# Order of work at the two seams between a LayerNorm stage and the feed-forward network of a hybrid decoder step

## What is computed

```python
def _swiglu(x, w_gate, w_up, w_down):
    return (jax.nn.silu(x @ w_gate) * (x @ w_up)) @ w_down

# layer 0: h = pooling mixer(x);  layer 1: h = latent attention(x) @ wo
x = _layer_norm(ALPHA * x + h, ln_g[l, 0], ln_b[l, 0])
x = _layer_norm(ALPHA * x + _swiglu(x, w_gate[l], w_up[l], w_down[l]), ln_g[l, 1], ln_b[l, 1])
```

## Time and profile before

| | |
|---|---|
| median of three runs | 2610.28 us |
| the profiled execution | 2611.03 us |
| its span, first to last instruction | 2609.2 us |
| mean granted TensorE clock | 0.969 |
| TensorE busy | 2415.3 us (93%) |
| VectorE busy | 1294.6 us (50%) |
| ScalarE busy | 769.7 us (30%) |
| GpSimd busy | 347.1 us (13%) |
| share of the chain that ended last, TensorE | 80% |

### The profile page before, as it was taken

How to read it: one execution, slowest core, us unless ns; L and a number is a source line. 1 busy time by engine, 2 the same in 40 slices (tenths; PEclk the granted TensorE clock), 3 DMA queues, 4 the chain that set the end, 5 groups by cost and what they waited for, 6 DMA issues and landing times.

```text
span 2609.2 us, 35320 instructions
## 1 busy us (share of the span) xinstructions
PE 2415.3 (93%) x14022; PEld 2198.0 (84%) x14022; DVE 1294.6 (50%) x2467; ACT 769.7 (30%) x1469; POOL 347.1 (13%) x308
## 2 busy tenths in 40 slices
PE   7899999999999768999998888898999999999994
PEld 7799999999999667898987667687999989999993
DVE  4623433333333765677767778643234434433336
ACT  2331111111111233555546556412311111111112
POOL 2400000000000330000006545032000000000006
PEclk9899999999999888999999999899999999999997
DMA  4021111111111031000004444500211111101111
GB/s 158 26 65 49 49 48 35 29 48 48 48 49 41 20 121 44 18 14 5 11 21 158 155 152 152 179 25 25 65 49 49 34 49 49 50 30 36 49 41 65
DMA packets 137082, 153.99 MB, mean 59 GB/s; under 512 B 10256, under 2 KB 114224, under 8 KB 136808
## 3 DMA queue, kind: packets, MB, share of 16 engines
q1 hardware_dynamic: 124656, 110.07, 13.4%
q0 software_dynamic: 12288, 41.95, 5.1%
HBM read 142.24 MB, written 10.32 MB: 58 GB/s over the span
## 4 chain that ended last, share of the span: by engine, by line
PE 80%; DVE 9%; ACT 4%; issue 3%; POOL 2%; DMA 2%; SPq 0%; POOLq 0%; ACTq 0%; DVEq 0%
PE ps L214 23%; PE ps L216 22%; PE ps L215 22%; DVE split L207 4%; ACT split L202 2%; PE ps L2010 2%; PE ps L2045 2%; POOL plain L338 1%; POOL plain L340 1%; PE ps L2025 1%; PE ps L222 1%; PE ps L221 1%; PE ps L2026 1%; PE ps L2032 1%; PE ps L1555 1%
## 5 line engine op out<-in xcount | busy, mean ns | idle before, releaser
L214 PE MATMUL ps<-split 128*128 128x512 f32 (+6 forms) x3632 | 1244.5, 343 | 69.9 <-DVE split L207 23.6
L215 PE MATMUL ps<-split 128*128 128x512 f32 (+6 forms) x3632 | 1229.2, 338 | 0.0
L216 PE MATMUL ps<-split 128*128 128x512 f32 (+6 forms) x3632 | 1228.1, 338 | 0.0
L214 PEld LDWEIGHTS ps<-split 128*128 128x128 f32 x3632 | 694.5, 191 | 120.1 <-DVE split L207 28.9
L216 PEld LDWEIGHTS ps<-split 128*128 128x128 f32 x3632 | 694.8, 191 | 38.0
L215 PEld LDWEIGHTS ps<-split 128*128 128x128 f32 x3632 | 694.8, 191 | 37.1
L202 ACT ACTIVATE split<-plain 128x1024 fp32r<-128x1024 f32 (+8 forms) x446 | 313.3, 738 | 628.7 <-PE ps L222 406.1
L207 DVE TENSOR_TENSOR split<-plain,split 128x1024 fp32r<-128x1024 f32 (+7 forms) x422 | 355.7, 867 | 193.1 <-ACT split L202 190.2
L274 DVE TENSOR_TENSOR plain<-plain,ps 128x512 f32<-128x512 f32 (+2 forms) x396 | 268.6, 685 | 201.9 <-PE ps L216 196.6
L910 DVE TENSOR_TENSOR plain<-plain,ps 128x350 f32<-128x350 f32 (+1 forms) x132 | 68.1, 516 | 574.6 <-ACT plain L866 574.0
L207 DVE TENSOR_TENSOR split<-ps,split 128x512 fp32r<-128x512 f32 (+5 forms) x480 | 247.6, 555 | 153.9 <-ACT split L202 146.4
(11 more groups left out here) (145 smaller groups left out, 1427.1 us busy)
## 6 DMA issues: line engine op xcount, KB each, us to landing
plain<-w_gate SPq DMA_DIRECT2D x44, 512.0 KB, 4.7
plain<-w_up SPq DMA_DIRECT2D x44, 512.0 KB, 4.0
plain<-w_down SPq DMA_DIRECT2D x44, 512.0 KB, 4.4
plain<-x_prompt SPq DMA_DIRECT2D x8, 512.0 KB, 11.2
x_spill<-plain SPq DMA_DIRECT2D x1, 4096.0 KB, 18.6
plain<-wo SPq DMA_DIRECT2D x8, 512.0 KB, 4.9
plain<-x_spill SPq DMA_DIRECT2D x8, 512.0 KB, 7.7
y_prompt<-plain SPq DMA_DIRECT2D x8, 512.0 KB
```

What stands on the lines that cost most here:

```text
L214: pe.matmul(out, still[0], moving[0], start=start, stop=False)
L215: pe.matmul(out, still[0], moving[1], start=False, stop=False)
L216: return pe.matmul(out, still[1], moving[0], start=False, stop=stop)
```

## The change

- The first three gate-and-up products are placed in steps 8, 9 and 11 of the normalising stage, ahead of the transposes of those steps, and the order of the six products of step 0 is part by part: (slot 0, part 0), (slot 1, part 0), (slot 0, part 1), (slot 1, part 1), and so on. The first waits for the transposed tiles 0 to 2, the second for those to 5, the fifth for all.
- Products with even numbers take banks 2 and 3, those with odd numbers 0 and 1. In mix and att the ring of the transposes shrinks to banks 0 and 1; tiles 6 and 7 use 7 and 4, the tail 5, with waits for their earlier users.
- Tiles 2 and 3 of the weights are split in step 8 of the normalising stage. The Silu, multiplication and splits of the first two products are done in steps 10 and 11, ahead of the transposed tiles of those steps on ScalarE.
- Tiles 4 and 5 are split ahead of the sixth product's Silu, since slot 0 is now read until the fifth product.
- The nine residual scalings go in threes behind the fourth, fifth and sixth products' Silus.

```diff
-def turn_bank(k, t, b):
-    if t >= k.tiles - 1:
-        return 7 if t == k.tiles else 2 + b
-    return (2 * t + b) % TURN_BANKS
+def turn_bank(k, ph, t, b):
+    if ph == "ffn0":
+        if t >= k.tiles - 1:
+            return 7 if t == k.tiles else 2 + b
+        return (2 * t + b) % TURN_BANKS
+    if t >= k.tiles - 2:
+        return 5 if t == k.tiles else (7, 4)[b]
+    return b
+
+def pe_turn_free(pe, k, ph, t, b):
+    n = 2 * t + b
+    if ph == "ffn0":
+        if n >= TURN_BANKS:
+            pe.wait_ge(*k.s.at(ph + "_turned_lo", n + 1 - TURN_BANKS))
+        return
+    if t == k.tiles:
+        pe.wait_ge(*k.s.at(ph + "_unit_taken", 2 * k.tiles + 1))
+        return
+    if n == 2 * (k.tiles - 2) and ph == "mix":
+        pe.wait_ge(k.s["pooled_lo"], 2 * k.tiles + 1)
+    if n == 2 * (k.tiles - 2) + 1:
+        pe.wait_ge(*k.s.at(ph + "_unit_taken", 2 * k.tiles))
+    if n >= 2:
+        pe.wait_ge(*k.s.at(ph + "_turned_lo", n - 1))
...
     def between(step):
-        if step >= k.tiles + 2:
-            k.ffn[layer].first_product(pe, step - k.tiles - 2)
+        if step in FIRST_PRODUCTS:
+            k.ffn[layer].gate_up(pe, 0, FIRST_PRODUCTS.index(step))
     return between
+
+FIRST_PRODUCTS = (8, 9, 11)
+
+def first_hidden(k, eng, layer, step, act):
+    if step in (10, 11):
+        (k.ffn[layer].act_hidden if act else k.ffn[layer].dve_hidden)(eng, 0, 0, step - 10)
...
         if step == k.tiles - 2:
             k.ffn[layer].split_first(eng, act)
+        if step == k.tiles:
+            if layer == 1 and act:
+                eng.wait_ge(*k.s.at("att_unit_done", 2 * (k.tiles + 1)))
+            k.ffn[layer].split_gate_up(eng, 0, 2, 1, 1, act)
+        first_hidden(k, eng, layer, step, act)
...
+def gu_bank(g, m):
+    return (2, 0)[g % 2] + m
...
+        if isinstance(st, int) and st == 0:
+            return [(0, 0), (1, 0), (0, 1), (1, 1), (0, 2), (1, 2)]
+        return [(slot, p) for slot in range(2) for p in range(PARTS)]
...
-            eng.wait_ge(*self.k.s.at(self.name("gu_done"), PARTS * c - PARTS))
+            eng.wait_ge(*self.k.s.at(self.name("gu_done"), 5 if isinstance(c, int) and c == 2 else PARTS * c - PARTS))
...
-        if isinstance(st, int) and st == 0 and slot == 0:
-
-            pe.wait_ge(*k.s.at(self.x_ph + "_turned_lo", (2 * k.tiles - 2, 2 * k.tiles, 2 * k.tiles + 1)[p]))
+        slot, p = self.order(st)[g]
+        if isinstance(st, int) and st == 0:
+
+            if g == 0 and self.layer == 0:
+                pe.wait_ge(k.s["pooled_lo"], 2 * k.tiles + 2)
+            if g in (0, 1, 4):
+                pe.wait_ge(*k.s.at(self.x_ph + "_turned_lo", {0: 6, 1: 12, 4: 17}[g]))
...
         def body(st, par):
+            first = isinstance(st, int) and st == 0
+            for g in range(2 if first else 0, 2 * PARTS):
+                if g == 0:
+                    self.weights(act, st, 0, True)
+                if g == (5 if first else PARTS):
+                    self.weights(act, st, 1, True)
+                self.act_hidden(act, st, par, g)
+                if first:
+                    for t in ((), (), (), (0, 1, 2), (3, 4, 5), (6, 7, 8))[g]:
+                        scale_row(t)
```

More of the change, by code:

```diff
@@ L676, in h_view, with order, h_count @@
         return self.k.h_tail[:, par, slot, part * LO:part * LO + b - a]
-    def h_count(self, q):
-        chunk, r = q // PARTS, q % PARTS
-        return (PARTS + 1) * chunk + r + 1 + (r == PARTS - 1)
+    def order(self, st):
+        if isinstance(st, int) and st == 0:
+            return [(0, 0), (1, 0), (0, 1), (1, 1), (0, 2), (1, 2)]
+        return [(slot, p) for slot in range(2) for p in range(PARTS)]
+    def h_count(self, st, q):
+        if q < 0:
+            return q
+        return sum(len(self.pieces(p)) for _, p in self.order(st)[:q + 1])
     def steps_of(self, eng, body, last):
@@ L809, in gate_up @@
             for kc in range(k.kc):
-                mm = product(pe, ps[:, 2 * (g % 2) + m, 0:b - a],
+                mm = product(pe, ps[:, gu_bank(g, m), 0:b - a],
                              (self.wgu(st, slot, m, 0)[:, kc, :], self.wgu(st, slot, m, 1)[:, kc, :]),
@@ L841, in body @@
         def body(st, par):
[L842 to L845, removed]
+            for g in range(len(FIRST_PRODUCTS) if isinstance(st, int) and st == 0 else 0, 2 * PARTS):
+                self.gate_up(pe, st, g)
             if isinstance(st, int) and st == 0:
@@ L853, in pe, with act_hidden @@
                                                       self.layer == 0, self.latent_products(pe)))
+    def act_hidden(self, act, st, par, g):
+        k = self.k
+        slot, p = self.order(st)[g]
+        n = 2 * PARTS * st + g
+        a, b = self.part(p)
+        act.wait_ge(*self.k.s.at(self.name("gu_done"), n + 1))
+        if not (isinstance(n, int) and n < 2):
+            act.wait_ge(*self.k.s.at(self.name("h_mul"), n - 1))
+        act.activation(k.silu[:, g % 2, 0:b - a], k.ps[:, gu_bank(g, 0), 0:b - a], ACT.Silu).then_inc(self.s("silu"), 1)
+        act.wait_ge(*self.k.s.at(self.name("h_mul"), n + 1))
+        if not (isinstance(st, int) and st < 2) and g == 0:
+            act.wait_ge(*self.k.s.at(self.name("unit_done"), 18 * (st - 1)))
+        for piece in self.pieces(p):
+            hi_part(act, self.h_view(par, 0, slot, piece), k.hidden[:, g % 2, piece[1]:piece[2]])\
+                .then_inc(self.s("h_hi"), 1)
@@ L856, in act @@
     def act(self, act):
         k, nt = self.k, self.nt
[L859 to L875, removed]
@@ L877, in body, with scale_row @@
-        def body(st, par):
[L878 to L890, removed]
+        def scale_row(t):
+            row = rows_of(k, t, nt)
+            if t == 0:
+                act.wait_ge(*k.s.at(self.x_ph + "_turned", 17))
+            act.activation(row, row, ACT.Copy, scale=ALPHA).then_inc(self.s("x_scaled"), 1)
@@ L897, in act, with dve_hidden @@
         self.steps_of(act, body, last)
+    def dve_hidden(self, dve, st, par, g):
+        k = self.k
+        slot, p = self.order(st)[g]
+        n = 2 * PARTS * st + g
+        a, b = self.part(p)
+        dve.wait_ge(*self.k.s.at(self.name("silu"), n + 1))
+        if not (isinstance(n, int) and n < 2):
+            dve.wait_ge(*self.k.s.at(self.name("h_lo"), 2 * (PARTS + 1) * st + self.h_count(st, g - 2)))
+        dve.tensor_tensor(k.hidden[:, g % 2, 0:b - a], k.silu[:, g % 2, 0:b - a], k.ps[:, gu_bank(g, 1), 0:b - a],
+                          ALU.mult).then_inc(self.s("h_mul"), 1)
+        dve.wait_ge(*self.k.s.at(self.name("h_hi"), 2 * (PARTS + 1) * st + self.h_count(st, g)))
+        for piece in self.pieces(p):
+            lo_part(dve, self.h_view(par, 1, slot, piece), k.hidden[:, g % 2, piece[1]:piece[2]],
+                    self.h_view(par, 0, slot, piece)).then_inc(self.s("h_lo"), 1)
@@ L900, in dve @@
     def dve(self, dve):
         k, nt = self.k, self.nt
[L903 to L918, removed]
-        def body(st, par):
[L921 to L925, removed]
+        def body(st, par):
+            first = isinstance(st, int) and st == 0
+            for g in range(2 if first else 0, 2 * PARTS):
+                if g == 0:
+                    self.weights(dve, st, 0, False)
+                if g == (5 if first else PARTS):
+                    self.weights(dve, st, 1, False)
+                self.dve_hidden(dve, st, par, g)
```

27 lines of the change are left out of this document (9 added, 18 removed).

## The result

The changed kernel takes 2588.33 us (median of 5 runs, 2584.85 to 2591.22), the kernel before beside it 2610.28 us. The ratio is 0.9922, 95% interval 0.9909 to 0.9935. The profiled execution took 2584.85 us with a span of 2583.0 us.

A forecast was written before the change was run, and what follows sets the result against it. TensorE bounds the kernel, busy at full clock in the steady feed-forward, with waits and half clock at the two seams. Gains 5.1 + 8.5 + 4.9 + 4.9 = 23.4 us give 2587 us, range 2576 to 2600.

The forecast's parts named there:

- The clock: Seams: half clock costs 2.7 us at layer 0's second product, 1.5 at each layer's third, none at layer 1's second.
- Start of the second product: Layer 0's seam: starts at 109.6 us after 6.1 us idle, split pair 5.9 us; layer 1: 2.3 us idle.
- Start of the third: Both seams: released by the first product's multiplication, 5.3 us after tile 6's transposes begin; 122.6 us in layer 0.
- Start of step 1: Waits of 3.7 and 3.8 us go, 0.3 and 0.4 us are new; net gain 4.9 us in each layer.
- The ring of two banks at nothing: Transposes of tiles 1 to 5: no cost; without cover up to 1.3 us per tile, 13 us for ten tiles.
- The sum: Both seams and both starts of step 1: 5.1 + 8.5 + 4.9 + 4.9 = 23.4 us gained.
- A sign of being wrong that came: Layer 0: the forecast is wrong if step 0 lasts longer than 64 us.
- rival (c): Second product held by VectorE, early first product only fills idle time; some 5 us remain, 2605 us; chance 0.07.
- (a): Seams: the clock doesn't fall at the new waits; gain 29 us, 2581 us; chance 0.17.
- (b): Step 1: the wait stays, 1.9 us of slack eaten; about 10 us less gain, 2597 us; chance 0.12.
- (d): Both seams: clock stays at 1.2 GHz to the end of step 0; slower, 2658 us; chance 0.04.

The follow-up runs named there:

- experiment 3: Changed kernel with GpSimd's gain and bias of tile 6 in layer 0's mixer applied to 8 columns only; 2583.21 us, ratio 0.9897.
- experiment 9: Kernel of experiment 8 with weight tiles 2 and 3 split one step later, in step 9 instead of 8; 2581.30 us, ratio 0.9901.
- experiment 4: Changed kernel with odd products of step 0 in banks 4 and 7, transposes keeping banks 0 and 1 for all eight tiles; 2570.69 us, ratio 0.9854.
- experiment 5: Changed kernel with Silu, multiplication and splits of the first two products one step earlier (steps 9 and 10); 2577.86 us, ratio 0.9891.
- experiment 1: Kernel before with only the nine residual scalings in threes behind the fourth, fifth and sixth Silus; 2597.45 us, ratio 0.9956.
- experiment 2: Changed kernel with all nine scalings put back behind the sixth Silu of step 0; 2596.88 us, ratio 0.9957.
- experiment 8: Changed kernel with second product again of slot 0, part 1 and third of slot 1, part 0; 2589.00 us, ratio 0.9936.
- experiment 7: Changed kernel with edits of experiment 4 and experiment 5, and the third product moved ahead of tile 7's transposes; 2568.81 us, ratio 0.9851.

## Why the prediction was right, step by step

The forecast was 2587 us; 2588.33 was measured. The waits came out as worked out; the clock's part came out by errors that partly cancel, and in one place by luck. Its steps:

- **Start of the second product.** 109.6 forecast, 109.73 found; the pair 5.9 and 5.93; in layer 1 the wait 2.3 and 2.20. Experiments 3, 9 and 4 show the three links of it: GpSimd, VectorE's queue, and the banks. In experiment 4, with other banks, the same product starts without a wait.
- **Start of the third.** 5.3 us after tile 6's transposes begin; 5.2 found in both layers. Experiment 5 shows that ScalarE's queue makes 2.0 us of it.
- **Start of step 1.** Waits of 3.7 and 3.8 us gone, 0.3 and 0.4 new; 0.38 and 0.47 found. Experiments 1 and 2 give 11.5 and 9.9 us (22.0 less 12.1) for the scalings, where I had about 10.
- **The ring of two banks at nothing** in tiles 1 to 5: no wait there in either layer of the changed kernel. The cover is thin: in experiment 8, where TensorE was faster ahead of it, tile 4's transposes waited 0.88 us in layer 0.
- **The clock is where sizes were off.** I gave the second product of layer 0 2.7 us, it lost 1.65 (9.35 less 7.7). I gave each third product 1.5, they lost 2.85 and 2.86 (10.55 less 7.7, 10.46 less 7.6). Together 7.4 us for 5.7. I had taken the loss by the length of the idle time before it; that was not the measure (next section but one). That the second product of layer 1 lost nothing behind 2.20 us, as I had assumed, was luck of this execution: in experiments 2, 5 and 8 it lost 1.5 us behind the same wait.
- **The sum.** Layer 0: 10.0 us forecast, 9.6 found. Layer 1: 13.4 and 11.3, of which 1.4 are the clock behind the third product and 0.6 the loop's own idle time. In all 23.4 and 20.9.
- **A sign of being wrong that came.** I had written that step 0 of layer 0 must not last longer than 64 us. It lasted 64.2 us in the window above and 64.5 from its first product, for some 63.8 that the sum gives. The waits there were as forecast; the excess is mostly the clock, 1.35 us more than forecast at the third product and 1.05 us less at the second.
- **Two readings.** The wait in step 1 of layer 0 stands 15.56 us into the step (182.71 less 3.70 less 163.45), not 15.4, which changes nothing of weight. And rival (c) was priced too low: 5 us left out the scalings, which give 11.5 us alone (experiment 1).

Of the rivals, (a), a clock that stays up, was false at three places of four; experiment 7 shows what it would have taken in layer 1. (b) was false: the multiplication of step 1's first product was done at 172.0 us, some 2.5 us before TensorE came to the third, for 1.9 us forecast. (c) was false as a whole, since experiment 2 keeps 12.1 us without the scalings. It held in one thing: most of the 7.7 us that the early first product filled in layer 0 came back as the wait of 6.43 us, and experiments 4 and 9 get it out. (d) was false: each fall ended inside the product that followed.

## What to carry to other kernels

When a product is moved forward, its start is set by the slowest in-order queue among its inputs, and the resource it shares (here two PSUM banks) can tie it to a queue that its data does not need: give it other banks, or move the work ahead of it in that queue behind it. Work that is needed later, like the nine scalings, belongs in small pieces into the idle time of its engine, and never in one block ahead of a split that a load waits for. Before placing a VectorE subtraction of two SBUF operands, look where GpSimd's long operations lie: here it cost the subtractions 3.6 us in one place and 1.9 in another.

## What the runs showed that I had not expected

The loss of clock does not follow the length of the last wait. A single wait of 1.07 us (experiment 5) or 1.57 (experiment 9) cost nothing, but 1.58 us ahead of the tail's transposes in experiment 7 cost 1.6. Among the longer ones, 2.92 us (experiment 3) cost 1.7, and 6.43 us no more, 1.65. Two short pieces, 1.07 and 1.96 us with tile 7's transposes between them, cost 2.85 us. The same two pieces (1.07 and 2.03) in layer 1 of experiment 4 cost only 1.7: 9.29 us to the tail's transposes, less 7.6.

Nor does the same wait cost the same each time. Layer 1's second product behind its wait of 2.20 us, in the changed kernel and then in that of experiment 2 (granted clock third from last, 1.00 and 0.81):

```profile
1777.04:1784.70 7.66, 7.66 (x49) 7.64 (x50) 0.95 (x5) 0.00 (x0) 4.77 (x2) 1.00 0.01 2
```

```profile
1783.78:1792.96 9.18, 9.18 (x48) 9.16 (x49) 0.95 (x5) 0.00 (x0) 4.72 (x2) 0.81 0.01 2
```

The five kernels that have this wait split into two with no loss (the changed kernel and experiment 3) and three with 1.5 us (experiments 2, 5 and 8). And the clock can be down with no wait at all: from 78.5 to 94.5 us, in the mixer's last units ahead of layer 0's seam, TensorE was busy all 16 us in the changed kernel, yet the clock was 0.68; in experiment 8 it was 1.00 there. I have no rule that gives all of these, so a single profile does not settle what the clock costs at a wait.

Layer 1's feed-forward has idle time that no engine releases, at up to three places some 140 us apart, as many as its loop goes back. Waits for nobody on TensorE from 1870 to 2490 us, in the changed kernel and in that of experiment 4:

```profile
PE ps L214 <- issue: 5.3, 3, 1.8
```

```profile
PE ps L214 <- issue: 2.8, 2, 1.4
```

Over the eleven kernels profiled it came to between 2.8 and 5.3 us, and layer 0's loop, which has the same form, shows none. It goes with the loading of instructions. The DMA queue marked "instruction" moved 36 packets of 16 KB from 1870 to 2490 us in each of the nine kernels with three such pieces, 27 in the two with two pieces, and 9 or 10 from 200 to 840 us in layer 0. So the engines fetch their program again when layer 1's loop goes back; that TensorE waits for just that is likely but not shown, and why one return in three was sometimes spared, and layer 0's loop always, is open.

The stretch between the seams varied by 6.5 us besides. The runs of the kernel before scatter over 12.3 us; that this and the loop's returns make up much of that is a guess from single executions of different kernels. What makes that stretch vary stays open.
